# Moving the merge gate's projection out of a recurrence's slots and into a block-product stage, in a hybrid mLSTM and pooling layer

## The reference

```python
parts = split((rmsnorm(x) * (1 + scale) + shift) @ in_w)   # q k v o z_m gates p z_p g_branch
# two scans over 16 chunks of 128 tokens, one per direction, 4 heads each, after 2 chunks of context
h   = num / max(|den|, exp(-m))                            # one chunk of one head and direction
h_x = h_forward + h_backward
y_m = (headnorm(h_x) * w * sigmoid(o) * silu(z_m)) @ branch_m_w
y_p = (pooled(p) @ pool_w * pool_scale * silu(z_p)) @ branch_p_w
g_m, g_p = split(g_branch)                                 # 1024 columns each
out = rmsnorm(x + gate * ((sigmoid(g_m) * y_m + sigmoid(g_p) * y_p) @ out_w))
```

## Time and profile before

| | us |
|---|---|
| executions | 2370.75, 2377.28, 2377.03 |
| median | 2377.03 |
| span of the profiled execution, first to last instruction | 2369.2 |
| TensorE busy | 2250.3 (95%) |
| VectorE busy | 1545.0 (65%) |
| ScalarE busy | 992.4 (42%) |
| GpSimd busy | 651.1 (27%) |
| projection stage | about 93 to 987 |
| scan stage | about 992 to 1837 |
| last stage | about 1840 to 2369 |

### The profile page before, as it was taken

How to read it: one execution, slowest core, us unless ns; L and a number is a source line. 1 busy time by engine, 2 the same in 40 slices (tenths; PEclk the granted TensorE clock), 3 DMA queues, 4 the chain that set the end, 5 groups by cost and what they waited for, 6 DMA issues and landing times.

```text
span 2369.2 us, 35117 instructions
## 1 busy us (share of the span) xinstructions
PE 2250.3 (95%) x12107; PEld 1907.1 (80%) x12107; DVE 1545.0 (65%) x2616; ACT 992.4 (42%) x2022; POOL 651.1 (27%) x558
## 2 busy tenths in 40 slices
PE   7799999998999999899999998999999798999998
PEld 5588888786778888778888887888888687888878
DVE  5554567757466675466877685888877455656564
ACT  6323345435233333334444444444544535352532
POOL 0233444533333443222322321232222112020200
PEclk9899999999999999999999999999999999999999
DMA  9466688767466765568777779877678665747562
GB/s 277 144 157 165 186 234 255 224 145 227 122 184 177 203 175 131 176 204 264 246 237 252 259 240 318 267 262 244 217 261 276 197 200 160 240 157 233 178 206 98
DMA packets 405442, 497.46 MB, mean 210 GB/s; under 512 B 25832, under 2 KB 291604, under 8 KB 400788
## 3 DMA queue, kind: packets, MB, share of 16 engines
q1 hardware_dynamic: 334740, 377.76, 48.3%
q10 hardware_dynamic: 62688, 83.90, 14.5%
q0 software_dynamic: 7840, 33.56, 4.9%
...
## 4 chain that ended last, share of the span: by engine, by line
PE 39%; DVE 7%; ACT 4%; issue 4%; DMA 3%; SPq 1%; DVEq 0%; POOL 0%; ACTq 0%
PE bank L1926 18%; PE bank L2550 9%; PE bank L1884 3%; PE bank L2605 3%; PE bank L1897 3%; PE bank L1905 2%; PE bank L1874 1%; ACT junk_h L2665 1%; ACT hsum L2675 1%; DMA v_t<-vk_d 1%; DVE state L2093 1%; DVE wl L2789 1%; DVE wl L2098 1%; DVE yt L2806 1%; ACT wh L2657 1%
## 5 line engine op out<-in xcount | busy, mean ns | idle before, releaser
L1926 PE MATMUL bank<-xlate,wh 128*128 128x512 f32 x1536 | 512.2, 405 | 6.9 <-DVE v_t L2070 4.9
L1031 PE MATMUL bank<-xlate,wh 128*128 128x512 f32 x1280 | 410.0, 396 | 5.8 <-DVE wl L1308 3.8
L1926 PEld LDWEIGHTS bank<-xlate,wh 128*128 128x128 f32 x1536 | 279.8, 190 | 56.7 <-DVE v_t L2070 5.3
L1031 PE MATMUL bank<-xtop,wh 128*128 128x512 f32 x960 | 307.1, 397 | 7.7 <-ACT wh L1083 4.0
L1926 PE MATMUL bank<-xlate,wl 128*128 128x512 f32 x768 | 310.8, 405 | 0.0
L1031 PEld LDWEIGHTS bank<-xlate,wh 128*128 128x128 f32 x1280 | 239.1, 189 | 59.1 <-issue 7.0
L1031 PE MATMUL bank<-xlate,wl 128*128 128x512 f32 x640 | 251.5, 393 | 0.0
L1031 PEld LDWEIGHTS bank<-xtop,wh 128*128 128x128 f32 x960 | 178.3, 189 | 47.1 <-ACT wh L1083 7.6
L1336 DVE SCALAR_TENSOR_TENSOR tmp<-bank,psum 128x512 f32<-128x512 f32 x144 | 99.1, 688 | 146.4 <-PE bank L1031 106.0
L1031 PE MATMUL bank<-xtop,wl 128*128 128x512 f32 x480 | 189.2, 394 | 0.0
L1926 PEld LDWEIGHTS bank<-xlate,wl 128*128 128x128 f32 x768 | 145.9, 190 | 24.5
...
## 6 DMA issues: line engine op xcount, KB each, us to landing
...
q_t<-qk_d SPq DMA_DIRECT2D x128, 256.0 KB, 4.1
...
rawb<-in_in_w_dram ACTq DMA_DIRECT2D x80, 256.0 KB, 5.6
wraw<-in_in_w_dram ACTq DMA_DIRECT2D x76, 256.0 KB, 4.1
...
k_t<-qk_d SPq DMA_DIRECT2D x64, 256.0 KB, 4.7
```

The source lines that it names most:

```text
L1031: mm = pe.matmul(dst[:, :], a[:, kd, :], x_block(part, XB[name])[:, kd], start=(kd == 0 and n == 0), stop=(kd == KH - 1 and n == 2))
L1926: mm = pe.matmul(bank[m % 2][:, :], a[:, u % 2, k, :], xlate[part][:, BLOCK_OF[k // KH, tq], k % KH], start=(k == 0 and n == 0), stop=(k = ...
```

## The change

The kind m leaves the scan. Its 1024 columns become eight units of a new kind "m" in the projection stage, four for each half of the tokens, right behind the four p units of that half and handled like them (tanh, store to `gm_d`). The scan keeps 64 pieces of kinds o and z, 1536 matmuls. Its slots get uneven shares, 10 to 13: 71 slots take about 9.9 matmuls each, the other 65 about 12.8. The six scores now follow six single matmuls in a row, from the fourth of the slot on. In the first half the division of num moves from VectorE to ScalarE, behind wexp of the next slot, with a semaphore of its own (`h_made`) for the store. `tanh_z` has three buffers in place of one. Only 8 column pairs go through `wpair_d`. `zpq` is loaded in four parts, each behind the store of one of the last four z pieces, since z now ends the scan's pieces.

```diff
--- before.py
+++ after.py
@@ -71,7 +71,7 @@
-    SCAN_COLS = [off + 2 * P * n for off in (O0, Z0, GM0) for n in range(KT // 2)]
+    SCAN_COLS = [off + 2 * P * n for off in (O0, Z0) for n in range(KT // 2)]
@@ -597,9 +597,9 @@
-            UNITS = [(0, i, kind) for kinds in ("vk", "qs", "p") for i in range(HEADS) for kind in kinds]
+            UNITS = [(0, i, kind) for kinds in ("vk", "qs", "p", "m") for i in range(HEADS) for kind in kinds]
...
-            UNITS += [(1, i, kind) for i in range(1, HEADS) for kind in "qs"] + [(1, i, "p") for i in range(HEADS)]
+            UNITS += [(1, i, kind) for i in range(1, HEADS) for kind in "qs"] + [(1, i, kind) for kind in "pm" for i in range(HEADS)]
@@ -646,7 +646,7 @@
-                return kind_of(a) == "p"
+                return kind_of(a) in "pm"
...
@@ -811,7 +811,7 @@
-                    sp.dma_start(gp_d[2 * i + e, :, t0:t0 + TQ], s_slot(which)).then_inc(s_stored[which], 16)
+                    sp.dma_start((gm_d if kind == "m" else gp_d)[2 * i + e, :, t0:t0 + TQ], s_slot(which)).then_inc(s_stored[which], 16)
@@ -1091,7 +1091,7 @@
-                        c0 = {"q": Q0, "k": K0, "v": V0, "p": GP0}[kind] + i * HD
+                        c0 = {"q": Q0, "k": K0, "v": V0, "p": GP0, "m": GM0}[kind] + i * HD
...
@@ -1581,9 +1581,8 @@
-            tanh_z = sb("tanh_z", [P, TQ])
+            tanh_z = sb("tanh_z", [P, 3, TQ])
...
-            gstage = sb("gstage", [P, 2, TQ])
@@ -1620,13 +1619,13 @@
-            pw_loaded = sem("pw_loaded"); zpq_loaded = sem("zpq_loaded"); mixq_loaded = sem("mixq_loaded")
+            pw_loaded = sem("pw_loaded"); zpq_loaded = [sem(f"zpq_loaded{n}") for n in range(2)]; mixq_loaded = sem("mixq_loaded")
...
-            g_stored = [sem(f"g4_stored{n}") for n in range(2)]
+            h_made = sem("h_made")
@@ -1649,7 +1648,7 @@
-            KINDS = "ozm"
+            KINDS = "oz"
@@ -1665,14 +1664,14 @@
-            ng = [sum(p[2] == "m" for p in PIECES[:m]) for m in range(NPI + 1)]
...
-            cut = [t * NPI * NMM // NSLOT for t in range(NSLOT + 1)]
+            SHARE = [10 if t < LEAD + NHALF - 1 else 13 for t in range(NSLOT)]
+            cut = [sum(SHARE[:t]) * NPI * NMM // sum(SHARE) for t in range(NSLOT + 1)]
@@ -1769,14 +1768,16 @@
-                    elif kind == "m":
-                        sp.wait_ge(act_read, na[m] + 1)
-                        sp.dma_start(gm_d[trip % (NTRIP // 2) * 2 + e, :, t0:t0 + TQ],
-                                     gstage[:, ng[m] % 2, :]).then_inc(g_stored[ng[m] % 2], 16)
+
+                def first_zp(m):
+                    trip, u, kind, e, tq = PIECES[m]
+                    if kind == "z" and trip == NTRIP - 1:
+                        g = 2 * e + tq
+                        sp.dma_start(zpq[:, g], zp_d[g, :, 0:TQ]).then_inc(zpq_loaded[tq], 16)
...
-                    sp.wait_ge(fin, 4 * (l + 1))
+                    sp.wait_ge(h_made, l + 1)
@@ -1831,6 +1832,7 @@
+                        first_zp(m)
@@ -1843,16 +1845,12 @@
-                    if t == HEAD_AT + 4:
-
-                        sp.wait_ge(u_made, nz[-1])
-                        sp.dma_start(zpq[:, :, :], zp_d[:, :, 0:TQ].rearrange("g p t -> p g t")).then_inc(zpq_loaded, 16)
...
+                    first_zp(m)
...
-                    sp.wait_ge(g_stored[n], 16 * ng[-1] // 2)
@@ -1890,7 +1888,7 @@
-                        pe.wait_ge(fin, 4 * (l - 1) + 1)
+                        pe.wait_ge(fin, 3 * (l - 1) + 1)
@@ -1938,11 +1936,11 @@
-                        if 0 <= l + 1 < NHALF and i % 2 == 1 and 2 <= i // 2 < 2 + len(SCORES):
-                            if i == 5:
+                        if 0 <= l + 1 < NHALF and i >= 3 and i - 3 < len(SCORES):
+                            if i == 3:
...
-                            score(l + 1, i // 2 - 2)
-                        if t < LEAD and i % 8 == 7 and i // 8 < CPS - 1:
+                            score(l + 1, i - 3)
+                        if t < LEAD and i % 5 == 4 and i // 5 < CPS - 1:
@@ -2008,14 +2006,13 @@
-                        if nz[m] >= 1:
-                            act.wait_ge(z_read, nz[m])
-                        act.activation(tanh_z[:, :], bank[m % 2][:, :], ACT.Tanh, scale=0.5).then_inc(dz, 1)
-                    else:
-                        a = ng[m]
-                        if a >= 2:
-                            act.wait_ge(g_stored[a % 2], 16 * (a // 2))
-                        act.activation(gstage[:, a % 2, :], bank[m % 2][:, :], ACT.Tanh, scale=0.5).then_inc(act_read, 1)
+                        if nz[m] >= 3:
+                            act.wait_ge(z_read, nz[m] - 2)
+                        act.activation(tanh_z[:, nz[m] % 3, :], bank[m % 2][:, :], ACT.Tanh, scale=0.5).then_inc(dz, 1)
+
+                def normalise(l):
+                    act.wait_ge(fin, 3 * l + 3)
+                    act.activation(num[:, l % 2, 0:HD], num[:, l % 2, 0:HD], ACT.Copy, scale=den[:, l % 2, 1:2]).then_inc(h_made, 1)
@@ -2026,6 +2023,8 @@
+                    if 0 <= l - 1 < NHALF:
+                        normalise(l - 1)
@@ -2058,7 +2057,7 @@
-                            act.wait_ge(fin, 4 * (l - 1) + 1)
+                            act.wait_ge(fin, 3 * (l - 1) + 1)
@@ -2131,7 +2130,7 @@
-                    dve.scalar_tensor_tensor(out=ustage[:, a % 2, :], in0=tanh_z[:, :], scalar=1.0, in1=bank[m % 2][:, :],
+                    dve.scalar_tensor_tensor(out=ustage[:, a % 2, :], in0=tanh_z[:, a % 3, :], scalar=1.0, in1=bank[m % 2][:, :],
@@ -2147,18 +2146,16 @@
-                    dve.wait_ge(fin, l * 4 + 1)
+                    dve.wait_ge(fin, l * 3 + 1)
...
-                    dve.wait_ge(fin, l * 4 + 2)
+                    dve.wait_ge(fin, l * 3 + 2)
...
-                    dve.wait_ge(fin, l * 4 + 3)
-                    if l < NHALF:
-                        dve.tensor_scalar(num[:, L, 0:HD], num[:, L, 0:HD], den[:, L, 1:2], None, ALU.mult).then_inc(fin, 1)
-                    else:
+                    if l >= NHALF:
+                        dve.wait_ge(fin, l * 3 + 3)
...
-                                                 in1=hother[:, L, :], op0=ALU.mult, op1=ALU.add).then_inc(fin, 1)
+                                                 in1=hother[:, L, :], op0=ALU.mult, op1=ALU.add).then_inc(h_made, 1)
@@ -2818,8 +2815,7 @@
-                        if g == 0:
-                            dve.wait_ge(zpq_loaded, 16)
+                        dve.wait_ge(zpq_loaded[g % 2], 32)
...
```

4 lines of the change are left out of this document (2 added, 2 removed).

## The result

The changed kernel takes **2423.9 us** (median of 4 runs, 2419.1 to 2427.7) against 2377.2 us for the kernel before beside it (2370.8 to 2378.3): a ratio of **1.021, 95% interval 1.019 to 1.023**. It is slower by 47 us where the prediction said 30; 2423.9 lies inside the range.

What follows compares the result with a forecast made beforehand. TensorE was taken to bound the kernel, with VectorE close behind in the scan. Terms +153.2 + 1 - 96 - 19 - 9 gave +30 us, 2399 on the profiled span; 7.8 for the median made 2407 us, range 2368 to 2440.

Steps and rivals of the forecast that it cites:

- Added in the projection: Projection stage: eight new units of 84 matmuls cost +153.2 us, with the other engines' work hidden behind TensorE.
- Context slots: The eight context slots: each loses 7.06 matmuls, saving 9 us, within bounds of 0 and 12.9.
- The boundary: Scan's end to last stage: z's operations and the last zpq load lie behind the last piece, +1 us (0 to 5.5).
- First half: Scan's first half: slots fall from 6.60 to 5.10 us, a little above VectorE's demand of 4.95, saving 96 us.
- Second half: Scan's second half: VectorE becomes the bound, slots fall from 5.70 to 5.40 us, saving 19 us.
- The allowance over the demand: Scan: slots taken a little above VectorE's demand, 5.10 over 4.95 and 5.40 over 5.33 us, since single waits don't average out.
- Transfers: Scan: 176 MB in some 670 us need 263 GB/s, against 260 and 253 before, so they cost nothing.
- Rival C: Scan: loads asked three slots ahead get less time, the mid-scan reload reaches TensorE; some 10 us more, 2417; chance within forecast's 0.54.
- Rival B: Scan: VectorE's collision with GpSimd locks in every late slot, slots of 5.30 and 5.60 us, +60 us, 2437; chance 0.20.
- p_l "at or above 0.65": Scan: a sign that the forecast is right, the mean time of VectorE's p_l staying at or above 0.65 us.
- The division: First half: moved to ScalarE, it costs 0.05 us a slot there and takes 22.9 us off VectorE's demand.
- The clock: Scan: TensorE's granted clock, 0.99 and 1.00, left alone because waits would be only some tenths of a microsecond.

Runs made afterwards that it cites:

- the four buffers: The changed kernel with four buffers in place of two for the scan step's result (num, den): 1.0191 of the kernel before.
- the release: The changed kernel with GpSimd's operation of a slot released only after VectorE's p_l of that slot: 1.0081 of the kernel before.
- the spread: The changed kernel with each quarter's mid-scan reload of token blocks sent two transfers per slot over four slots: 1.0223 of the kernel before.

## Why the prediction was right in its direction and short in size

The sum said +30 and the spans differ by 54.9: 25 short, of which the terms below make up 14.5, 12.6 and 4.2, less 6.1 and 0.5. (The medians differ by 47, as the new span does not lie below its median as the old one does. The 7.8 us that the forecast added for that did not come, so by luck the forecast of 2407 misses the time by 17 us and not by 25.)

**Added in the projection, +153.2.** Right per unit: the new units take 19.23 us each, 153.8 for eight, with TensorE full. That the others' work costs nothing held, and more: three of the older units became 6.4 us shorter, so the stage grew by 147.1. Not foreseen, and no run takes it apart.

**Context slots, -9.** Measured -9.5.

**The boundary, +1.** Measured +5.2, near the upper bound of 5.5. Of it 3.8 us are busy time of TensorE for the same 2880 matmuls (491.7 us, 487.9 before) at a granted clock of 0.97 instead of 0.98; the rest no run takes apart.

**First half, 5.10 us a slot, -96.** Measured 5.32, -81.5: 14.5 short. **Second half, 5.40, -19.** Measured 5.60, -6.4: 12.6 short. The demand was read rightly: VectorE is late, the idle time before the state's update is 4.1 us in the second half, TensorE's wait put down to den is 63.8 us (up to 40 had been said). (Counts of wl were a little off: wh stands 23 times in each half of before, not 22 and 24, which is worth 0.04 us a slot.) The allowance over the demand was not what failed. Without the three slots of about 15 us the means are (340.6 - 14.6) / 63 = 5.17 and (353.0 - 29.9) / 61 = 5.30 us, near the 5.10 and 5.40 of the forecast.

**Transfers, nothing: the step that failed.** The working compared mean rates, 260 and 253 GB/s with 263, but the price lies in bursts. The three slots in which num waits for a store stand some 29 us above the others (9.4 and 19.3 us by the means just given). Before there was one, of 14.8 us, 8 us above its neighbours' mean of 6.47. The difference, some 20 us, is most of the 27 that the halves are short. Rival C (some 10 us) was on this track, with the reload, but it looked for the wait at TensorE's loads and had half its size. What the burst costs by itself stays open, as a wait taken away comes back at its next user: the four buffers gave 5 us alone, within the intervals, and 10 with the release, and the spread nothing.

**Rival B's own working** had slots of 5.30 and 5.60 and +60, five us from the 54.9 of the spans. Its cycle is in the trace (5.16 us at 1670 us; length + 3.6 forecast), but its way to the sum is not, so the agreement of the means is luck. It let every late slot collide, with p_l near 1.2 us and slots with z and wl near 7; measured are p_l of 0.394 and 0.792 us on the mean, and 5.4 and 5.2 us for the slots with z or wl (those above 9 left out). Of the forecast's own signs, p_l "at or above 0.65" failed in the first half: the division's leaving took p_l out of GpSimd's way there, and with it back p_l is 0.675. With the later release the slots are 5.11 and 5.29, but that is not the forecast come true, since the forecast had left the collisions in VectorE's demand.

**The division, 0.05 us a slot on ScalarE** and 22.9 us of demand less. Against the run with the division back, VectorE's work is 35 us less, but the half only 7.4 us shorter (348.0 to 340.6). A demand read as "all time but the slack" counts waits that come back when something else is removed.

**The clock, left alone.** It stands at 0.98 and 0.96 in the halves (0.99 and 1.00 before). The plain slots, with waits of tenths of a microsecond, run at 1.00, as said; but the change also brought waits of TensorE of up to 9.1 us, and with them more stretches at 0.50 (1.2 GHz), some 40 us in the halves where it had been 10. Counting half of TensorE's busy time in these stretches as lost, an estimate, they cost 13 us in the halves instead of 3, and 10 instead of 6 in the last stage. A granted clock of 0.70 behind the one long wait was in the rows; that there would be more such waits was not in the sum.

**Why no version of the move wins.** By 0.228 us a matmul the move trades 175.1 us for 153.2, a profit of 21.9. Measured, TensorE's busy time fell by 143.5 us in the halves and 13.9 in the context slots and rose by 150.0 in the projection: 7 us are left. By the same estimate the clock is about half of the difference; the rest is open. So the move wins only if TensorE idles hardly more in the scan than it did, and even with GpSimd's long operations gone it idles 30 us in the halves instead of 15; that kernel is level with the one before.
